# Loop order of the projection blocks: contraction chunk, then pass, then the three token tiles

## The reference, cut to what matters

```
h = h + rmsnorm(y)                               # y: conv mixer (layer 0) or attention (layer 1)
h = h + rmsnorm(swiglu(rmsnorm(h), w_gate, w_up, w_down))
h = h + sigmoid(h @ w_ple_gate) * (p @ w_ple)

swiglu(x) = (silu(x @ w_gate) * (x @ w_up)) @ w_down      # 1024 -> 2816 -> 1024
```

## Time and profile before

| | |
|---|---|
| time, median of 3 runs | 3643.12 us (3639.33 to 3643.56) |
| span of the profiled execution | 3636.2 us |
| own time of the profiled execution | not given apart; 3643.12 - 3636.2 = 6.9 us is what the median has beside the span |
| PE busy | 3391.7 us, 93% |
| weight loads (PEld) busy | 3149.3 us, 87% |
| DVE, ACT, POOL busy | 45%, 24%, 6% |
| mean granted TensorE clock | 0.970 |
| matmuls of lines 1540 to 1542 | 18% of the chain that ended last for each line |

### The profile page before, as it was taken

The page is one execution under the profiler, slowest core; times in us unless marked ns, Lnnn a source line. Parts: engine busy times, 40 slices in busy tenths (PEclk is TensorE's granted clock), DMA queues, the critical chain, the costliest instruction groups (busy, mean ns, idle before and its releaser), DMA issues.

```text
span 3636.2 us, 52786 instructions
## 1 busy us (share of the span) xinstructions
PE 3391.7 (93%) x19908; PEld 3149.3 (87%) x19908; DVE 1632.8 (45%) x2755; ACT 863.6 (24%) x1465; POOL 211.3 (6%) x379
## 2 busy tenths in 40 slices
PE   7999889999999968999889999999799999999977
PEld 6999779999999968999788865556689999999977
DVE  5444463443344565433467732222553433343562
ACT  3111131111111223222355621112231111111221
POOL 1000000000000000000211112220000000000000
PEclk9999999999999989999999999999899999999988
DMA  2111101111111111132322245552101111111111
GB/s 86 46 40 47 41 24 47 46 40 46 46 40 46 47 41 30 41 114 62 96 50 59 47 164 186 186 162 76 35 29 47 43 46 47 41 47 42 56 33 55
DMA packets 222916, 225.57 MB, mean 62 GB/s; under 512 B 10725, under 2 KB 183781, under 8 KB 222770
## 3 DMA queue, kind: packets, MB, share of 16 engines
q1 hardware_dynamic: 196994, 146.82, 13.2%
q0 software_dynamic: 25776, 76.63, 7.0%
HBM read 196.92 MB, written 18.10 MB: 59 GB/s over the span
## 4 chain that ended last, share of the span: by engine, by line
PE 87%; DVE 6%; ACT 2%; issue 2%; DMA 1%; POOL 0%; POOLq 0%; ACTq 0%; DVEq 0%; SPq 0%
PE psum L1542 18%; PE psum L1540 18%; PE psum L1541 18%; PE psum L1555 5%; PE psum L1561 5%; PE psum L1556 5%; PE psum L1931 3%; PE psum L1845 3%; PE psum L1835 2%; PE psum L1894 2%; PE psum L1977 2%; PE psum L1956 2%; DVE psum L1032 1%; DVE y L1038 1%; DVE h L1048 1%
## 5 line engine op out<-in xcount | busy, mean ns | idle before, releaser
L1540 PE MATMUL psum<-xs_hi,w_hi 128*128 128x384 f32 (+1 forms) x2736 | 892.9, 326 | 7.1 <-DVE y L1247 4.0
L1542 PE MATMUL psum<-xs_hi,w_lo 128*128 128x384 f32 (+1 forms) x2736 | 892.3, 326 | 0.0
L1541 PE MATMUL psum<-xs_lo,w_hi 128*128 128x384 f32 (+1 forms) x2736 | 891.7, 326 | 0.0
L1540 PEld LDWEIGHTS psum<-xs_hi,w_hi 128*128 128x128 f32 x2736 | 513.6, 188 | 8.8 <-DVE y L1247 5.0
L1542 PEld LDWEIGHTS psum<-xs_hi,w_lo 128*128 128x128 f32 x2736 | 513.5, 188 | 0.0
L1541 PEld LDWEIGHTS psum<-xs_lo,w_hi 128*128 128x128 f32 x2736 | 513.5, 188 | 0.0
L1555 PE MATMUL psum<-xs_hi,w_hi 128*128 128x384 f32 (+1 forms) x1104 | 361.2, 332 | 10.1 <-DVE w_lo L1010 3.7
L1556 PE MATMUL psum<-xs_hi,w_lo 128*128 128x384 f32 (+1 forms) x1104 | 358.9, 330 | 0.0
L1542 PE MATMUL psum<-hid_hi,w_lo 128*128 128x384 f32 (+1 forms) x1056 | 346.0, 328 | 0.0
L1541 PE MATMUL psum<-hid_lo,w_hi 128*128 128x384 f32 (+1 forms) x1056 | 345.1, 327 | 0.0
L1540 PE MATMUL psum<-hid_hi,w_hi 128*128 128x384 f32 (+1 forms) x1056 | 344.7, 326 | 0.0
(11 more groups left out here) (263 smaller groups left out, 4185.9 us busy)
## 6 DMA issues: line engine op xcount, KB each, us to landing
kpage<-in_cache_k SPq DMA_DIRECT2D x64, 512.0 KB, 4.9
v_page<-in_cache_v POOLq DMA_DIRECT2D x128, 256.0 KB, 3.4
raw<-in_w_gate SPq DMA_DIRECT2D x44, 512.0 KB, 3.7
raw<-in_w_up SPq DMA_DIRECT2D x44, 512.0 KB, 3.7
raw<-in_w_down SPq DMA_DIRECT2D x44, 512.0 KB, 3.4
raw<-in_w_in SPq DMA_DIRECT2D x24, 512.0 KB, 3.7
raw<-in_w_ple_gate SPq DMA_DIRECT2D x16, 512.0 KB, 4.0
out<-rows_out POOLq DMA_DIRECT2D x16, 512.0 KB, 2.9
```

Of the source, the lines that this page charges most:

```text
L1540: M(out, wh, xh, start=first, stop=False)
L1541: M(out, wh, xl, start=False, stop=False)
L1542: return M(out, wl, xh, start=False, stop=last)
```

## The change

The blocks of `block8` that have their activations ready, and the blocks of `down`, are written in another order. Before: tile, then chunk, then the three passes. Now: chunk, then pass, then the three tiles, so that three matmuls in a row have the same weights and go to three banks. All three banks of a block are claimed at its start, and they are complete together at its end. `tile_in_parts`, the per-layer embedding, the first block of `w_out` and everything on the other engines are unchanged.

```
+            def tiles_under_weights(outs, wh, wl, xh, xl, c, first, last):
+
+                for (t0, n), out in zip(TILES, outs):
+                    M(out, wh, xh[:, c, t0:t0 + n], start=first, stop=False)
+                for (t0, n), out in zip(TILES, outs):
+                    M(out, wh, xl[:, c, t0:t0 + n], start=False, stop=False)
+                for (t0, n), out in zip(TILES, outs):
+                    ins = M(out, wl, xh[:, c, t0:t0 + n], start=False, stop=last)
+                    if last:
+                        ins.then_inc(acc_ready, 1)
...
-                for t, (t0, n) in enumerate(TILES):
-                    pe.wait_ge(acc_free, blk * NT + (t + 1))
-                    if xs0 is not None:
+                if xs0 is not None:
+                    for t, (t0, n) in enumerate(TILES):
+                        pe.wait_ge(acc_free, blk * NT + (t + 1))
                         tile_in_parts([(acc(par, t), slot)], xh, xl, xs0, t)
-                        continue
-                    for c in range(C):
-                        k = slice(c * P, (c + 1) * P)
-                        ins = three(acc(par, t), w_hi[slot][:, k], w_lo[slot][:, k],
-                                    xh[:, c, t0:t0 + n], xl[:, c, t0:t0 + n], c == 0, c == C - 1)
-                    ins.then_inc(acc_ready, 1)
+                    return
+                pe.wait_ge(acc_free, blk * NT + NT)
+                for c in range(C):
+                    k = slice(c * P, (c + 1) * P)
+                    tiles_under_weights([acc(par, t) for t in range(NT)], w_hi[slot][:, k], w_lo[slot][:, k],
+                                        xh, xl, c, c == 0, c == C - 1)
...
-                            for t, (t0, nn) in enumerate(TILES):
-                                pe.wait_ge(acc_free, blk * NT + ((4 * s + m) * NT + t + 1))
-                                for c in range(2):
-                                    k = slice(c * 512 + m * P, c * 512 + (m + 1) * P)
-                                    ins = three(acc(m, t), w_hi[s][:, k], w_lo[s][:, k],
-                                                hid_hi[par][:, c, t0:t0 + nn], hid_lo[par][:, c, t0:t0 + nn],
-                                                c == 0, c == 1)
-                                ins.then_inc(acc_ready, 1)
+                            pe.wait_ge(acc_free, blk * NT + ((4 * s + m) * NT + NT))
+                            for c in range(2):
+                                k = slice(c * 512 + m * P, c * 512 + (m + 1) * P)
+                                tiles_under_weights([acc(m, t) for t in range(NT)], w_hi[s][:, k], w_lo[s][:, k],
+                                                    hid_hi[par], hid_lo[par], c, c == 0, c == 1)
```

## The result

The changed kernel takes 3680.8 us (median of 4 runs, 3678.2 to 3685.7), the kernel before 3643.3 us on the same chip (3639.3 to 3655.9). The ratio is 1.009, 95% interval 1.0068 to 1.0113, so 25 to 41 us slower; forecast were +26 us and 3669 us. The profiled execution took 3679.34 us, its span is 3677.7 us. The ratios and intervals here leave out slow executions; among all the runs there was one, of e12 (6841.9 us).

What follows compares the result with a forecast made beforehand. The prediction took TensorE's matmul stream, busy 93%, as the bound. Terms 12 + 12 + 2 = +26 us on 3643.1 gave 3669 us; own range 3655 to 3695, 8 in 10 range 3643 to 3725.

Steps and rivals of the forecast that it cites:

- Parts 1 and 2: In the changed blocks' matmuls, using weights three times in a row and taking three banks in turn each change 0.
- Part 3: In the changed blocks' triples, width changing at every third matmul costs 5 ns per triple, net +12 us.
- Rival A: In the triples, no price for width, as the disturbance needs a run of equal widths: 3651 us, chance 0.20.
- Rival B: In the triples, each pays the full 22 ns for its width change: 3731 us, chance 0.15.
- Part 4: At a down's third block after a gate_up, PE waits for three banks completing together: 20 x 0.6 = +12 us.
- Part 5: After w_out and the two feed-forwards, a norm waits 0.6 us longer for the last additions: +2 us.
- The 6.9 us: For the whole kernel, the median of the runs was taken as 6.9 us above the profiled span.
- Rival C: In the triples, matmuls that repeat weights come sooner, 13 ns each for two of three: 3557 us, chance 0.07.

Runs made afterwards that it cites:

- e12: The kernel before, unchanged, profiled and timed once more against the kernel before: ratio 1.0004.
- e5: The kernel before with the third tile's matmuls in the changed blocks widened to 384 columns, 64 of them not read: 3740.8 us.
- e6: The changed kernel with the third tile's matmuls in the changed blocks widened to 384 columns, 64 of them not read: 3750.2 us.
- e11: The changed kernel with token tiles of 384, 352 and 352 columns instead of 384, 384 and 320: 3662.1 us.
- e7: The changed kernel with its two inner loops exchanged, so chunk, then tile, then the three passes: 3671.4 us.
- e3: The changed kernel with VectorE making the low part of a down's second slab after the first down block's additions, not before: 3676.8 us.
- e8: The changed kernel with the new order only in the blocks of block8, the down blocks as in the kernel before: 3663.8 us.
- e9: The changed kernel with the new order only in the down blocks, block8 as in the kernel before: 3655.3 us.

## Why the prediction was right, and where it was off

- **Parts 1 and 2, weights and banks: 0.** Right. There are as many loads as matmuls in the changed kernel, and e5 and e6 agree to 0.01 us in 49.92.
- **Part 3, the width term: +12 forecast, +18.5 measured.** The term that was mis-sized is "five ns per triple": it is 6.7 (500.0 - 493.3). Five was picked between two bounds and not derived, so that it came near is in part luck, and the picture behind it, that the price builds up over the wide matmuls alone, is wrong: in the changed kernel more than half of it stands at the 320-column matmuls (150.5 ns on average for 146.7). From the windows: 84 gate and up blocks x (48.00 - 47.44) / 4 = 11.8, 22 downs x (24.00 - 23.84) = 3.5, 23 blocks of `w_out`, `w_q` and `w_v` x 0.14 = 3.2. The bounds were -42 and +74. Rival A (no price) is out for 384 and 320 columns; its "no price" is seen only with e11's widths. Rival B (22 ns per change, however short the run) is out: a change down and up costs 20 ns with six wide matmuls in a row (e7) and 6.7 with two.
- **Part 4, the wait: +12 forecast, +10 measured.** The forecast times were met within 0.13 us at every step, the wait stands at 20 places and no other, and e3, e6, e8 and e9 move it as the sum says: it is gone without the slab's low part ahead of the additions and without either half, and is 0.25 us where the block is longer.
- **Part 5, stage ends: +2 forecast, 1.5 measured.** PE's idle time before the norm of `w_out` is 3.88 us for 3.39, and before the transposes after each feed-forward 1.28 for 0.79, 3 x 0.49.
- **The sum.** 18.5 + 10 + 1.5 = 30 us. The changed kernel's span is 33.3 us over that of e12, which has all its turn waits too. Of the 3 us left 2.5 stand in the first blocks of `w_k`, which the change does not touch: the same 170 matmuls with the same 3.71 us of idle time ran at a granted clock of 0.87 and of 0.95 (first the changed kernel, then e12):

```profile
1463.76:1500.00 36.24, 32.53 (x170) 32.27 (x171) 26.20 (x50) 11.83 (x27) 0.00 (x0) 0.87 0.09 25
```
```profile
1449.85:1483.58 33.73, 30.02 (x170) 29.75 (x171) 26.22 (x50) 11.86 (x27) 0.00 (x0) 0.95 0.06 16
```

The unchanged kernel's two executions differ there too, 35.30 and 33.73 us. Against the first profile of the kernel before the difference is 41.5 us; 8 of these were the state of that execution. The medians' 37.5 us have an interval of 25 to 41. The 6.9 us that the forecast added to the span is not a fixed part either: in the runs here the time is 1.6 to 2.8 us above the span of the same execution, and the rest of the 6.9 is that the profiled execution was a quick one.
- **Rival C** had 0.07 and got nothing, as the pair 1540/1541 said.

What stays open is why a mixture of widths costs what it does. Shown are the prices: 384 and 320 alternating 6.7 ns per triple, 384 and 352 none or 6.7 less than none, 362 and 364 in either order 4 to 9 ns above 493.3 per three. "The distance of two starts depends on the widths around it" is a description and not a cause, and my two rules for it (equal widths settle; the price goes with the step) both failed. The steady sums of a triple that the traces show, 486.7, 493.3, 500.0 and 520.0 ns, are 73, 74, 75 and 78 times 6.67 ns; that is a hint at a step in the timing of matmuls, and no run tests it.

## What to carry to other kernels

Writing matmuls so that the same weights stand side by side saved nothing here, where every matmul has its own load and the loads are hidden under the stream; look for the load records of a pair that shares its weights before hoping for it. Completing several banks together costs the slack between them: lay the consumer's queue out from the moment of completion, instruction by instruction, and the wait can be forecast closely (here within 0.13 us at each step). Before a few microseconds in one trace are put down to a change, profile the unchanged kernel twice.

## What the runs showed of the hardware that was not expected

- Nearly equal tiles (362, 362, 364) are slower than 384, 384, 320 in the old order: 47.76 against 47.44 us per gate group, and the distances do not settle.
- In a settled stream 384 columns come every 173.3 ns and 320 every 146.7, that is N / 2.4 + 13.3 ns at a granted clock of 1.00. The Trainium skill, "TensorE: Matmul & The Clock Gate", section "Back-to-back issue gap", gives N / 2.4 + 2.5 ns for a matmul taken without its weight load, and less than that at large N for a stream with loads; the rows are above both, and they decide.
- The order of widths alone changes PE's throughput by 1.2% (47.44 to 48.00 us) without an idle time that any view shows; PE's busy share stays at 93%.
- One stream of 384, 352 and 352 columns ran at 493.3 ns per three in fifteen gate groups of e11 and at 486.7 in three, at the same granted clock.
- At the turn of the feed-forward loop the distance of two starts of PE is 0.8 to 1.3 us longer in the kernel before, but not always; the same program shows this at 4 turns in one execution and at 8 in another, together with more packets of the instruction queue (113 and 148).
